# Prompt attention with its value product swapped, its division in a copy, its heads written out, and its query blocks in the order long, short, long, short

## What is computed

```python
def fox_attend(q, c_q, pos_q, k, v, c_k, pos_k):
    s = jnp.einsum('bqhd,bkhd->bhqk', q, k).astype(jnp.float32) * (HEAD_DIM_B ** -0.5)
    bias = jnp.transpose(c_q, (0, 2, 1))[:, :, :, None] - jnp.transpose(c_k, (0, 2, 1))[:, :, None, :]
    mask = pos_k[None, :] <= pos_q[:, None]
    s = jnp.where(mask[None, None], s + bias, -jnp.inf)
    p = jax.nn.softmax(s, axis=-1)
    return jnp.einsum('bhqk,bkhd->bqhd', p.astype(v.dtype), v)
```

## Time and profile before

| | |
|---|---|
| median of 3 runs | 2880.69 us (2878.28 to 2882.22) |
| the profiled execution | 2881.99 us |
| its span | 2880.2 us |
| PE busy | 2716.2 us (94% of the span) |
| PE weight loads | 2593.0 us (90%) |
| DVE / ACT / POOL busy | 1341.1 / 746.9 / 397.0 us |
| granted clock of PE, mean over the span | 0.953 |
| largest groups | L665, L666, L667 (the large products), some 1100 us each for the tiles AH and AL |
| value product of prompt attention, L849 | 720 instructions, 92.9 us |

### The profile page before, as it was taken

How to read it: one execution, slowest core, us unless ns; L and a number is a source line. 1 busy time by engine, 2 the same in 40 slices (tenths; PEclk the granted TensorE clock), 3 DMA queues, 4 the chain that set the end, 5 groups by cost and what they waited for, 6 DMA issues and landing times.

```text
span 2880.2 us, 39704 instructions
## 1 busy us (share of the span) xinstructions
PE 2716.2 (94%) x15813; PEld 2593.0 (90%) x15813; DVE 1341.1 (47%) x1988; ACT 746.9 (26%) x1274; POOL 397.0 (14%) x401
## 2 busy tenths in 40 slices
PE   8999698888989999999999999998999999999996
PEld 7998577655889999999999999998999999999996
DVE  4788655311466333333333564376633232333356
ACT  3111455433225111111111252233411111111124
POOL 3298122200031000000000220012000000000022
PEclk9999798877799999999999999999999999999998
DMA  7110200222111111111111131120111111111101
GB/s 220 48 44 15 82 1 15 77 89 95 71 30 52 44 45 38 45 45 45 44 44 44 44 100 45 44 105 20 59 45 44 38 45 38 44 45 44 45 15 62
DMA packets 165307, 152.27 MB, mean 53 GB/s; under 512 B 8609, under 2 KB 140049, under 8 KB 165144
## 3 DMA queue, kind: packets, MB, share of 16 engines
q1 hardware_dynamic: 157632, 133.92, 15.2%
q0 software_dynamic: 6208, 15.94, 1.7%
q10 hardware_dynamic: 1320, 0.24, 0.1%
HBM read 131.43 MB, written 18.93 MB: 52 GB/s over the span
## 4 chain that ended last, share of the span: by engine, by line
PE 89%; DVE 5%; issue 3%; ACT 2%; DMA 1%; SPq 0%; ACTq 0%; DVEq 0%; POOL 0%; POOLq 0%
PE PS L665 25%; PE PS L666 25%; PE PS L667 25%; PE PS L849 3%; PE PS L905 2%; PE PS L836 1%; PE PS L817 1%; PE PS L821 1%; PE PS L887 1%; PE PS L679 1%; DVE SPR L1585 1%; PE PS L680 1%; DVE RSD L1761 1%; PE PS L673 0%; DVE SSM L1588 0%
## 5 line engine op out<-in xcount | busy, mean ns | idle before, releaser
L665 PE MATMUL PS<-AH,WHI 128*128 128x368 f32 x3360 | 1125.2, 335 | 26.3 <-issue 12.8
L666 PE MATMUL PS<-AL,WHI 128*128 128x368 f32 x3360 | 1118.2, 333 | 3.9 <-issue 3.9
L667 PE MATMUL PS<-AH,WLO 128*128 128x368 f32 x3360 | 1114.6, 332 | 0.0
L665 PEld LDWEIGHTS PS<-AH,WHI 128*128 128x128 f32 x3360 | 638.1, 190 | 34.7 <-issue 15.3
L667 PEld LDWEIGHTS PS<-AH,WLO 128*128 128x128 f32 x3360 | 637.4, 190 | 4.4 <-issue 4.4
L666 PEld LDWEIGHTS PS<-AL,WHI 128*128 128x128 f32 x3360 | 637.2, 190 | 2.9 <-issue 0.8
L1853 DVE TENSOR_TENSOR HF<-S,PS 128x368 f32<-128x368 f32 x132 | 70.9, 537 | 705.6 <-ACT S L1098 705.6
L665 PE MATMUL PS<-HH,WHI 128*128 128x368 f32 x1056 | 350.1, 332 | 3.2 <-DVE Y L1864 3.2
L666 PE MATMUL PS<-HL,WHI 128*128 128x368 f32 x1056 | 349.9, 331 | 0.0
L667 PE MATMUL PS<-HH,WLO 128*128 128x368 f32 x1056 | 349.6, 331 | 0.0
L1864 DVE TENSOR_TENSOR Y<-Y,PS 128x368 f32<-128x368 f32 x480 | 251.3, 535 | 156.7 <-PE PS L667 156.7
(11 more groups left out here) (258 smaller groups left out, 2402.6 us busy)
## 6 DMA issues: line engine op xcount, KB each, us to landing
RAW<-in_w_ffn_gate SPq DMA_DIRECT2D x44, 512.0 KB, 4.0
RAW<-in_w_ffn_up SPq DMA_DIRECT2D x44, 512.0 KB, 4.9
RAW<-in_w_ffn_down SPq DMA_DIRECT2D x44, 512.0 KB, 3.4
RAW<-in_w_in_even SPq DMA_DIRECT2D x20, 512.0 KB, 4.9
Y<-x_spill SPq DMA_DIRECT2D x16, 552.0 KB, 5.5
KR<-in_cache_k SPq DMA_DIRECT2D x32, 256.0 KB, 3.3
VR<-in_cache_v SPq DMA_DIRECT2D x32, 256.0 KB
RAW<-in_w_in_odd SPq DMA_DIRECT2D x16, 512.0 KB, 4.3
```

The source lines that it names most:

```text
L665: pe.matmul(out, wh, xh, start=first, stop=False)
L666: pe.matmul(out, wh, xl, start=False, stop=False)
L667: return pe.matmul(out, wl, xh, start=False, stop=last)
```

## The change

The value product has its operands swapped: PT (128 keys x 128 queries) becomes the weights and V (128 keys x 64 channels) is streamed, so the result has queries on partitions and 64 channels in its columns. Two banks take it in turn, 2 for even units and 7 for odd. With queries on partitions the division by the row sum is one factor per partition, so ACT does it in its copy of the result, into a new tile ATT, and POOL's pass over PB goes; `turn` waits for exp alone. ATT holds, for a pair of heads, 128 channels per query; it is transposed back (`back`, on PE, bank 7) and copied to QKV by DVE. 26 of the 36 transposes stand at the end of steps of later units (`BACKS`), the last 10 after all units (`LATE`), with banks 7 and 2 in turn. The two hardware loops are gone: all 72 units stand in the program, and each head's operands are made during the head before. Only the first head's are made ahead. `ORDER` puts long and short blocks in turn. Since scores of block 8 take three banks, they wait until the value result four units earlier has left bank 2, and value products of even units wait until exp of the last block 8 has read it.

```diff
-ORDER = (tuple(range(9)), (0, 8, 1, 2, 3, 4, 5, 6, 7))
+ORDER = ((7, 0, 6, 1, 5, 2, 4, 3, 8), (7, 8, 0, 6, 1, 5, 2, 4, 3))
...
+        ATT, o = at("ATT", B0 + 8 * T * 4, [P, 2, NTT, P])
...
+        BACKS = {18 * (jj + 1) + 5 + 2 * i: (jj, i) for jj in range(HT - 1) for i in range(NTT)}
+        LATE = [BACKS[n] for n in BACKS if n >= 75] + [(HT - 1, i) for i in range(NTT)]
...
-            with gp.Fori(0, 2) as it:
-                for a, h2, j, i, m, n, _, _ in ATT:
-                    gp.wait_ge(rc_ready, 36 * it + a + 1)
-                    gp.nop(nofuse=True)
-                    gp.tensor_scalar(PB[0:m, a % 3, 0:n], PB[0:m, a % 3, 0:n], ST4[0:m, 2, a:a + 1], 1.0,
-                                     ALU.mult, ALU.mult).then_inc(pn_ready, 1)
-
             gp.wait_ge(att_evac, 1 + 72)
+            gp.wait_ge(back_evac, HT * NTT)
...
+                pe.wait_ge(exp_done, u + 1)
+                if i == 8 and u > 3:
+                    pe.wait_ge(att_evac, u - 2)
...
-                pe.wait_ge(pn_ready, 36 * it + a + 1)
+                pe.wait_ge(exp_done, u + 3)
...
-                pe.wait_ge(att_evac, 36 * it + a + 1)
+                if u > 1:
+                    pe.wait_ge(att_evac, u)
+                if u % 2:
+                    if backs_until(u + 2):
+                        pe.wait_ge(back_evac, backs_until(u + 2))
+                elif wide_until(u + 3) >= 0:
+                    pe.wait_ge(exp_done, wide_until(u + 3) + 3)
                 for jt in range(i + 1):
                     kw = min(P, TP - jt * P)
-                    mm = pe.matmul(PS[0:HD, 7, 0:m], VP[0:kw, j, jt, HD * h2:HD * (h2 + 1)], PT[0:kw, a % 2, jt, 0:m],
-                                   start=(jt == 0), stop=(jt == i))
+                    mm = pe.matmul(PS[0:m, (2, 7)[u % 2], 0:HD], PT[0:kw, u % 2, jt, 0:m],
+                                   VP[0:kw, h // 2 % 2, jt, HD * (h % 2):HD * (h % 2 + 1)], start=(jt == 0), stop=(jt == i))
                 mm.then_inc(pv_done, 1)
...
+            def back(jj, i, bank=7, left=0, units=0):
+                x, m = NTT * jj + i, P if i < 8 else META
+                pe.wait_ge(att_evac, 1 + max(units, 18 * (jj + 1)))
+                if x > left:
+                    pe.wait_ge(back_evac, x - left)
+                pe.transpose(PS[:, bank, 0:m], ATT[0:m, jj % 2, i, :], IDN[0:m, 0:m]).then_inc(back_done, 1)
+
+            for n in range(72 + 3):
+                if n < 72:
+                    scores(*UNITS[n])
+                if 2 <= n < 74:
+                    turn(*UNITS[n - 2])
+                if n >= 3:
+                    values(*UNITS[n - 3])
+                if n in BACKS:
+                    back(*BACKS[n], units=n - 3)
+            for k, x in enumerate(LATE):
+                back(*x, bank=(7, 2)[k % 2], left=1 if k else 0, units=72)
...
+            def result(u, h, i, m, n, na, nb):
+                if u % 18 == 0 and u > 18:
+                    act.wait_ge(back_done, NTT * (u // 18 - 1))
+                act.wait_ge(rc_ready, u + 1)
+                act.wait_ge(pv_done, u + 2)
+                act.activation(ATT[0:m, h // 2 % 2, i, HD * (h % 2):HD * (h % 2 + 1)], PS[0:m, (2, 7)[u % 2], 0:HD], ACT.Identity,
+                               scale=ST4[0:m, 2, u:u + 1]).then_inc(att_evac, 1)
```

More of the change, by code:

```diff
@@ L1189, in head_high @@
                                     (0, QS2[0:HD, h2, :], HD ** -0.5))[part]
[L1190 to L1206 removed]
+                act.activation(out, QKV[own, h // 2 + tile, 0:TP], ACT.Copy, scale=scale).then_inc(qk_hi, 1)
+            for part in range(4):
+                head_high(0, part)
+            for n in range(72 + 3):
+                if n < 72:
+                    expo(*UNITS[n])
+                if 2 <= n < 74:
+                    turned(*UNITS[n - 2])
+                if n >= 3:
+                    result(*UNITS[n - 3])
+                if n < 63 and n % 9 in (2, 3, 4, 5):
+                    head_high(n // 9 + 1, n % 9 - 2)
+            act.wait_ge(back_evac, HT * NTT)
             act.wait_ge(cs_ready, 1)
@@ L1674, in _, with back, head_low @@
+            def back(jj, i, bank=7):
+                x, m = NTT * jj + i, P if i < 8 else META
+                dve.wait_ge(back_done, x + 1)
+                dve.tensor_copy(QKV[:, jj, i * P:i * P + m], PS[:, bank, 0:m]).then_inc(back_evac, 1)
             dve.wait_ge(ab_open, 1)
-            def head_low(it, x, part):
-                h2 = x % 2
+            def head_low(h, part):
+                h2 = h % 2
                 own, other = slice(HD * h2, HD * (h2 + 1)), slice(HD * (1 - h2), HD * (2 - h2))
@@ L1685, in head_low @@
[L1685 to L1701 removed]
+                    dve.wait_ge(qk_hi, 4 * h + 2)
@@ new lines, in head_low @@
+                    dve.scalar_tensor_tensor(QS1[other, h2, :], QKV[own, h // 2, 0:TP], HD ** -0.5, f32(QS1[own, h2, :]),
+                                             ALU.mult, ALU.subtract).then_inc(qk_lo, 1)
+                else:
+                    dve.tensor_scalar(QS2[64:96, h2, :], QBA[:], CST[0:32, K_MSK + h:K_MSK + h + 1], None, ALU.mult).then_inc(qk_lo, 1)
+            for part in range(3):
+                head_low(0, part)
+            for n in range(72 + 3):
+                if 1 <= n < 73:
+                    inverse(*UNITS[n - 1])
+                if n < 72:
+                    peak(*UNITS[n])
+                if 2 <= n < 74:
+                    turned(*UNITS[n - 2])
+                if n < 63 and n % 9 in (4, 5, 6):
+                    head_low(n // 9 + 1, n % 9 - 4)
+                if n in BACKS:
+                    back(*BACKS[n])
@@ L1704, in _ @@
+            for k, x in enumerate(LATE):
+                back(*x, bank=(7, 2)[k % 2])
             dve.wait_ge(t_done, TU_LFS + 1)
```

172 lines of the change are left out of this document (62 added, 110 removed).

## The result

| | before | after |
|---|---|---|
| median | 2878.28 us (2871.88 to 2882.22, 9 runs) | 2886.02 us (2882.73 to 2894.59, 9 runs) |
| ratio, 95% interval | | 1.003 (1.0019 to 1.0041) |
| the profiled execution | 2881.99 us | 2885.28 us |
| prompt attention, first score product to last value product | 224.2 us | 229.2 us |
| time without PE work in it | 13.8 us | 24.6 us |

The change makes the kernel slower by 0.3%: 7.7 us by the medians, 9 by the ratio. The sign, and the range from 2858 to 2945, held. The forecast of +15.6 us was about twice too much. Measured again beside later runs, the changed kernel stood at 1.003 (1.0016 to 1.0044) once more. (The window of the earlier trace rows is 0.4 us longer than the stage as counted here, hence 224.6 and 14.3 us there.)

What follows compares the result with a forecast made beforehand. PE, busy for 94% of the span, was taken to bound the kernel. Terms summed to +8.1 us at a steady clock and +7.5 for the clock, +15.6 in all: 2896 us against the median, range 2858 to 2945.

Steps and rivals of the forecast that it cites:

- New order, the main loss: Prompt attention with long and short blocks in turn: PE's value products wait for ACT's copy behind exp, +21 us (0 to 30).
- Swapped value product: 576 value instructions: weight loads set the pace, 0.112 us apart instead of 0.109, so half the columns buys nothing; +1.7 us.
- rival C: Value products: the load doesn't bind, 0.067 us apart in place of 0.112; -26 us, 2870 us; chance 0.04.
- Shape changes: All weights of a unit 128 wide, so three gaps on PE close: 0.29 us x 64 units, -18.6 us.
- Heads written out: PE's idle 5.8 us between the two turns of the head loop go, with filling and draining; -6.8 us.
- Clock: Granted PE clock in prompt attention: restart's slow stretch goes (-6.5), longer falls after block 8 (+9), new falls (+5); +7.5 us.
- Backs: 26 transposes back on PE within the steps, +2.8 us, up to 8; the last ten hidden before the samples' keys land.
- Division: POOL's division leaves the chain between exp and transposes and goes into ACT's result copy; 0 us.
- Bank 2: Scores of block 8 wait for ACT's copy of a value result, about 0.5 us, 16 times; +8 us (0 to 11).
- Rival A: Faster: the wait for ACT's copy doesn't appear (-21) and no more clock falls come (-14); 2861 us, chance 0.27.
- Rival B: Clock stays low: some 155 us of the stage instead of 55 at 1.2 GHz, +45; 2934 us, chance 0.17.
- Rival D: No difference: closed gaps, the idle 5.8 us and the new waits cancel; chance 0.12.

Runs made afterwards that it cites:

- a_copyfirst: The changed kernel with ACT's copy of the second half of a block's transposes put ahead of the exp of the unit two later; 2878.8 us, ratio 1.001.
- d_wide: `c_noswap_rising` with value-product weights of 128 columns for blocks 0 to 7, in the old orientation; 2846.0 us, ratio 0.9886.
- c_noswap_rising: The kernel before with its heads written out and nothing else of the change, blocks in the old order; 2855.2 us, ratio 0.9925.
- c_nodiv_rising: `c_noswap_rising` with POOL's division left out, so the output misses it; 2854.7 us, ratio 0.992.
- a_bank7: The changed kernel with all value results in bank 7, 26 transposes back behind their step's scores, their copies ahead of DVE's copy into PT; 2895.9 us, ratio 1.0065.
- a_wide_rising_b7: The changed kernel with 128 columns streamed in value products, old block order, all value results in bank 7, transposes back in bank 2; 2866.8 us, ratio 0.9968.
- a_wide: The changed kernel with value products streaming 128 columns, the values of both heads of a pair, instead of 64; 2873.9 us, ratio 0.999.

## Why the prediction was right in sign and wrong in its main term

My terms grouped as the runs can separate them (us, ratios times 2877):

| step | forecast | measured |
|---|---|---|
| heads written out, with the restart's time at 1.2 GHz | -6.8 - 6.5 = -13.3 | -22 |
| new order, its waits and its share of the clock | +21 and a part of +14 | +11 |
| swap, gaps, backs, bank 2, and the rest of the clock | -6.1 and a part of +14 | +20 |
| sum | +15.6 | +9 |

The step that failed is **"New order, the main loss"**, +21 us. It laid all of the loss on value products that wait for ACT's copy into PT. They wait 5.9 us in all, for any reason, and 1.2 us when that copy goes first (`a_copyfirst`). Part of the lateness that I had priced for block 5 is met ahead of the transposes (0.28 us there and 0.34 ahead of the values, in place of 1.1). And where I had counted four such waits in each of 8 heads, the stage has eleven ahead of value products, 0.3 to 0.9 us long; why the others stay away is open. The new order is a loss nevertheless, +11 by the ratios on top of written-out heads. The profiles show it in waits (17.3 against 5.7 us) and in time at 1.2 GHz (49.6 against 29.1), which at 0.45 for each of the latter would make 21 us; they overstate what the ratios give, and that is not explained.

That the sum came out right in sign is luck in good part. The heads gave 9 us more than forecast, the order took at least 10 less, and the swap with what belongs to it took at least 12 more; these misses cancel to 7.

- *Swapped value product*, +1.7 us: right in its pace, 0.112 us apart where it was 0.109; rival C is out. What the halved streaming cost lies in the clock, below.
- *Shape changes*, -18.6: the mechanism is right for two of the three gaps, and `d_wide` shows it by itself. The third, inside the first pair of scores, closed by only 0.02 of 0.10, and so it wasn't one of width: the second pair of a unit, with the same shapes, stands 0.237 us apart, the first still 0.316. What makes it is open. The three steps came to 0.23 us a unit, -15; with the step between the first two value products, which I had not priced, the total is 0.33 in short units and less in long ones, where waits lie in between. So the term was of the right size, in part for other gaps than those named.
- *Heads written out*, -6.8, and the restart under *Clock*, -6.5: mis-sized, -22 in place of -13.3. The restart showed 13.0 us at 1.2 GHz in my window and 17.1 in the clock records, and in `c_noswap_rising` the stretches at the start and behind the restart are shorter too; 30 us in all. That these hang on the loop, and not on chance in one execution, rests on one profile of each kernel.
- *Backs*, +2.8 in the stage: not refuted, 1 to 14 by the ratios. The last ten are not quite free: from the last value product to the turning of the keys it takes 10.1 to 11.5 us in the nine profiles with them and 9.2 to 10.1 in the ten without.
- *Division*, 0: right in the old order, shown by `c_nodiv_rising`; not tested in the new one.
- *Bank 2*, +8: 6.9 us, in 8 waits of up to 1.35 instead of 16 of 0.5. There is one block 8 in each of 8 heads, so 16 was a miscount, and the longer waits made up for it. That taking them away would give them back was not shown (`a_bank7`, `a_wide_rising_b7`).
- *Clock*, +7.5: the profile after has 61.1 us at 1.2 GHz, 59.1 before. That is no small term but two large ones that cancel: 30 us less by the heads, 32 more by the rest. Streaming 64 columns instead of 128 alone accounts for 34 us of time at 1.2 GHz (61.1 against 27.1 in `a_wide`), where I had put 20 for it and the waits together.

Rival A failed where it says that the clock would stay up without the pause: most of the wait did stay away, and the time is still above that of the kernel before. Its condition was nearly met, and it was the clock and other short waits that kept it from coming true. Rival B's mechanism is real, at 61 to 68 us of 1.2 GHz instead of 155. Rival D is near to what happened: gains and losses cancel but for 8 to 9 us, just over the 5.8 us that I had taken as the limit of what can be told.

## What to carry to other kernels

Price one edit at a time where a change bundles several: here one part (-22 us) paid for two that lost (+11 and +20), and the median showed only the remainder. Where the load of the weights sets PE's pace, halving the streamed columns buys nothing, and doubling them can be free; count time at 1.2 GHz in the stage before and after, and look at it as a term as large as the waits. Keep successive weights equally wide, which can be had by widening an operand instead of swapping it, but not for a product that streams few columns. Keeping such products apart removed three of four falls of the clock here; that it saves time isn't shown.

## What had not been expected of the hardware

- The same kernel with the same loads, waits and PE busy share ran 34 us less at 1.2 GHz in the stage (55 less in the old order) when its value products streamed 128 columns instead of 64, and was 9 to 11 us faster for it.
- Widening the weights of 144 products of 16 streamed columns from 64 to 128 cost 18 us, more than twice the 8 us of the longer load. The rest goes with 13 us more at 1.2 GHz (53.5 against 40.5) and is not wholly accounted for.
- Where the program is untouched, executions still differ. From the turning of the keys to the end the profiles took 2318.9 us (the changed kernel), 2309.5 (the same again), 2306.5 (`a_wide`), 2324.3 (`a_wide_rising_b7`). A stage's own length in one profile is also good to a few us only: 229.2 and 232.2 us for the same program.
